# Query-key scores as two weighted fp32r products, their low parts made on VectorE, and four more up tiles ahead of the gates

## The reference, cut to what matters

```python
qry = (xf @ w_q).reshape(t, PEER_HEADS, 2, PEER_HALF)     # 8 heads, two halves of 128
s1 = einsum('thd,hkd->thk', qry[:, :, 0], k1)             # 128 keys each
s2 = einsum('thd,hkd->thk', qry[:, :, 1], k2)
v1, i1 = lax.top_k(s1, 16); v2, i2 = lax.top_k(s2, 16)
cand = v1[..., :, None] + v2[..., None, :]                # 256 per head
top_v, top_c = lax.top_k(cand, 16)
gates = softmax(top_v); idx = e1 * 128 + e2
act = gelu(einsum('phkd,pd->phk', u_tab[idx], xb))
out = einsum('phk,phkd->pd', gates * act, v_tab[idx])
```

## Time and profile before

| what | value |
| --- | --- |
| three runs | 1452.3, 1454.21, 1452.57 us |
| profiled execution, first to last instruction (the page gives no other time of it) | 1451.0 us |
| PE busy | 1443.0 us, 99% |
| DVE, ACT, POOL busy | 77%, 53%, 31% |
| instructions | 22297 |
| HBM traffic | 237 GB/s over the span |

### The profile page before, as it was taken

How to read it: one execution, slowest core, us unless ns; L and a number is a source line. 1 busy time by engine, 2 the same in 40 slices (tenths; PEclk the granted TensorE clock), 3 DMA queues, 4 the chain that set the end, 5 groups by cost and what they waited for, 6 DMA issues and landing times.

```text
span 1451.0 us, 22297 instructions
## 1 busy us (share of the span) xinstructions
PE 1443.0 (99%) x7422; PEld 1202.6 (83%) x7422; DVE 1121.3 (77%) x1929; ACT 767.8 (53%) x1010; POOL 445.1 (31%) x208
## 2 busy tenths in 40 slices
PE   9999999999999999999999999999999999999999
PEld 8888887878788888888888888888888888888887
DVE  5979898876689999996999997355666666666665
ACT  7445787776645455555555555454444444444442
POOL 5867566347457778892000000000000000000000
PEclk9999999999999999999999999999999999999999
DMA  7544534457433666666888888979889888888883
GB/s 241 174 145 145 186 117 155 167 184 265 145 130 121 217 218 214 214 215 215 304 301 306 302 305 298 342 243 323 288 293 288 289 288 291 286 292 284 295 287 140
DMA packets 166708, 345.17 MB, mean 238 GB/s; under 512 B 13421, under 2 KB 78957, under 8 KB 164337
## 3 DMA queue, kind: packets, MB, share of 16 engines
q1 hardware_dynamic: 166640, 344.32, 70.3%
HBM read 268.76 MB, written 75.51 MB: 237 GB/s over the span
## 4 chain that ended last, share of the span: by engine, by line
PE 97%; ACT 1%; DVE 1%; DMA 0%; issue 0%; SPq 0%; ACTq 0%
PE ps L1293 32%; PE ps L1302 32%; PE ps L791 13%; PE ps L814 6%; PE ps L1331 4%; PE ps L1162 3%; PE ps L1001 1%; PE ps L1228 1%; PE ps L779 1%; PE ps L1011 1%; PE ps L1055 1%; PE ps L1235 1%; PE ps L863 1%; PE ps L839 0%; DMA xs<-in_x 0%
## 5 line engine op out<-in xcount | busy, mean ns | idle before, releaser
L1293 PE MATMUL ps<-hT_r,u_r 128*128 128x512 f32 x2048 | 470.3, 390 | 0.0
L1302 PE MATMUL ps<-v_r,w_pairs 128*128 128x512 f32 x2036 | 461.7, 389 | 0.0
L1293 PEld LDWEIGHTS ps<-hT_r,u_r 128*128 128x128 f32 x2048 | 382.8, 188 | 79.1
L1302 PEld LDWEIGHTS ps<-v_r,w_pairs 128*128 128x128 f32 x2036 | 382.1, 188 | 79.4
L2484 DVE TENSOR_TENSOR v_r<-vraw,v_r 128x1024 fp32r<-128x1024 f32 x128 | 156.8, 1225 | 147.3 <-ACT v_r L1804 147.3
L1804 ACT ACTIVATE v_r<-vraw 128x1024 fp32r<-128x1024 f32 x128 | 135.7, 1060 | 253.3 <-PE ps L1302 247.9
L506 POOL TENSOR_TENSOR w_r<-w_raw,w_r 128x1024 fp32r<-128x1024 f32 x85 | 222.6, 2625 | 150.7 <-ACT w_r L1410 104.9
L581 POOL TENSOR_TENSOR u_r<-uraw,u_r 128x1024 fp32r<-128x1024 f32 x60 | 173.3, 2901 | 41.8 <-ACT u_r L1731 41.7
L1750 ACT ACTIVATE act_stage<-ps 128x512 f32<-128x512 f32 x128 | 76.5, 598 | 181.3 <-PE ps L1293 181.2
L1731 ACT ACTIVATE u_r<-uraw 128x1024 fp32r<-128x1024 f32 x128 | 135.3, 1058 | 54.1 <-DMA uraw<-in_u 50.8
L1410 ACT ACTIVATE w_r<-w_raw 128x1024 fp32r<-128x1024 f32 x95 | 100.0, 1059 | 84.5 <-PE ps L814 33.1
(11 more groups left out here) (299 smaller groups left out, 1577.4 us busy)
## 6 DMA issues: line engine op xcount, KB each, us to landing
uraw<-in_u SPq DMA_DIRECT2D x128, 512.0 KB, 4.7
vraw<-in_v SPq DMA_DIRECT2D x128, 512.0 KB, 5.2
w_raw<-in_w SPq DMA_DIRECT2D x100, 512.0 KB, 3.5
acts_out<-act_stage SPq DMA_DIRECT2D x128, 256.0 KB, 2.3
gates<-stage SPq DMA_DIRECT2D x16, 2048.0 KB, 7.4
g_in<-gates SPq DMA_DIRECT2D x64, 512.0 KB, 6.6
act_in<-acts_out SPq DMA_DIRECT2D x128, 256.0 KB, 5.3
gates_pre<-pre_stage SPq DMA_DIRECT2D x24, 256.0 KB, 2.2
```

Of the source, the lines that this page charges most:

```text
L1293: ins = pe.matmul(bank(s % 2), u2[s][:, w, k * P:(k + 1) * P], hr4[:, w, k, :], start=i == 0, stop=i == 15, skip_group_check=True)
L1302: ins = pe.matmul(bank(2 * q + h), w2[:, s, w, q * P:(q + 1) * P], v2[s][:, w, h * BANK:(h + 1) * BANK], start=start and w == 0, stop=stop ...
```

## The change

Six things change.

1. The keys are split once into `keys_hi` (keys / 128, by ACT, two instructions of 1024 columns) and `keys_lo` (keys - 127 x keys_hi, by DVE, in two halves). Each query is split into `q_hi` (127/128 of it, by ACT's old copy with a scale) and `q_lo` (the query minus q_hi, by DVE, read from PSUM: `low_query`).
2. `key_scores` makes for each 128 tokens two fp32r products (q_hi with keys_hi, q_lo with keys_lo) in place of one fp32 product; `score_copy` multiplies by 128. It waits for `qk_lo`, which DVE raises, in place of `pq_out`, which ACT raises.
3. DVE's program has `low_query(2g + 2)` and `low_query(2g + 3)` behind the first list g, for g below 7, and the second half of the keys behind list 2.
4. Scores 14 and 15 stand behind up tiles 0 and 1 in place of before them; the others are spread in pairs over the even items.
5. `N_TOP` goes from 60 to 64, and with it `N_GATE` from 108 to 112: POOL makes the low parts of four more up tiles, and four fewer are left behind the gates. `EXP_AFTER`, `TURN_AFTER` and `EARLY` change, and the second half of the gate table for the second four down tiles is loaded 14 and 15 tiles behind `N_GATE` in place of 15 and 17.
6. POOL writes its index pattern after eight up tiles in place of before the first; three semaphores are shared with others, with the waits raised to match.

```diff
-N_TOP, PER_BLOCK = 60, 12
+N_TOP, PER_BLOCK = 64, 12
-EARLY = (N_GATE + 8, N_GATE + 12, N_GATE + 16)
+EARLY = (N_GATE + 6, N_GATE + 9, N_GATE + 12)
-SCORES_AFTER = {1: (0,), 3: (1, 2), 5: (3, 4), 7: (5, 6), 9: (7, 8), 11: (9, 10), 13: (11, 12), 14: (13,), 15: (14,)}
+SCORES_AFTER = {1: (0,), 2: (1,), 4: (2, 3), 6: (4, 5), 8: (6, 7), 10: (8, 9), 12: (10, 11), 14: (12, 13)}
+LATE_SCORES = (14, 15)
+KEYS_BEHIND = 2
-EXP_AFTER, TURN_AFTER = (12, 24, 36, 49), (23, 36, 48, 56)
+EXP_AFTER, TURN_AFTER = (14, 27, 39, 51), (27, 40, 52, 60)
...
-                elif q in (15, 17):
-                    part_of_g(1, 1, (q - 15) // 2 * NBLK // 2)
+                elif q in (14, 15):
+                    part_of_g(1, 1, (q - 14) * NBLK // 2)
...
-                pe.wait_ge(pq_out, g + 1)
+                pe.wait_ge(qk_lo, g + 2 + (g >= 2 * KEYS_BEHIND + 2))
                 at_least(pe, score_out, g - 1)
                 for t in range(TT):
-                    ins = pe.matmul(bank(4 + s % 2)[:, t * P:(t + 1) * P], qryT3[:, s, t * P:(t + 1) * P],
-                                    keysT3[:, g, :] if isinstance(g, int) else keysT[:, bass.ds(g * NKEYS, NKEYS)],
-                                    start=True, stop=True)
+                    c_ = slice(t * P, (t + 1) * P)
+                    for w, (q_, k_) in enumerate(((q_hi3, keys_hi3), (q_lo3, keys_lo3))):
+                        ins = pe.matmul(bank(4 + s % 2)[:, c_], q_[:, s, c_], k_[:, g, :], start=w == 0, stop=w == 1)
...
             for n in range(N_TOP):
                 up(n, n % 4)
+                if n < len(LATE_SCORES):
+                    key_scores(LATE_SCORES[n], LATE_SCORES[n] % 4)
                 if n in TURN_AFTER:
...
+            def high_keys(h):
+
+                c_ = slice(h * D, (h + 1) * D)
+                act.wait_ge(xa_keys_in, 32)
+                act.activation(keys_hi[:, c_], keysT[:, c_], ACT.Copy, scale=1.0 / SPREAD).then_inc(key_hi, 1)
+
             for n in range(I_PQ + 2, I_PQ + 4):
                 high_w(n, n % 4, back=4)
+            high_keys(0)
...
-                act.activation(qryT3[:, n % 4, :], bank(query_bank(n)), ACT.Copy).then_inc(pq_out, 1)
+                act.activation(q_hi3[:, n % 4, :], bank(query_bank(n)), ACT.Copy, scale=KEEP).then_inc(pq_out, 1)
...
+            def low_query(n):
+
+                dve.wait_ge(pq_out, n + 1)
+                dve.tensor_tensor(q_lo3[:, n % 4, :], bank(query_bank(n)), q_hi3[:, n % 4, :].bitcast(F32),
+                                  ALU.subtract).then_inc(qk_lo, 1)
+
+            low_keys(0)
+            low_query(0)
+            low_query(1)
             for g in range(2 * PH):
                 first_lists(g)
+                if g == KEYS_BEHIND:
+                    low_keys(1)
+                if g < PH - 1:
+                    low_query(2 * g + 2)
+                    low_query(2 * g + 3)
```

More of the change, by code:

```diff
@@ L276, in build @@
         mem_scaled = projT[:, 0:2048].rearrange("p (k t) -> p k t", t=MEM)
-        qryT3 = qryT.rearrange("p (g t) -> p g t", t=T)
         keysT3 = keysT.rearrange("p (g k) -> p g k", k=NKEYS)
+        q_hi3, q_lo3 = (x.rearrange("p (g t) -> p g t", t=T) for x in (q_hi, q_lo))
+        keys_hi3, keys_lo3 = (x.rearrange("p (g k) -> p g k", k=NKEYS) for x in (keys_hi, keys_lo))
         sb_v3 = sb_v.rearrange("p (t c) -> p t c", c=512)
@@ L416, in build @@
         rows_made, if_made, cols_turned, cols_out = sem("rows_made"), sem("if_made"), sem("cols_turned"), sem("cols_out")
-        conv_done, silu_done, x_far = sem("conv_done"), sem("silu_done"), sem("x_far")
+        conv_done, silu_done, far = sem("conv_done"), sem("silu_done"), sem("far")
         normed, qkT_lo, mpT_lo = sem("normed"), sem("qkT_lo"), sem("mpT_lo")
@@ L523, in _ @@
                     pool.tensor_scalar(x_scaled[:, n, :], side_of(xr4[:, 0], k, side).bitcast(F32), SPREAD - 1.0, 1.0,
-                                       ALU.mult, ALU.mult).then_inc(x_far, 1)
+                                       ALU.mult, ALU.mult).then_inc(far, 1)
             for n in range(2, 6):
@@ L574, in _, with low_us @@
             low_ws(I_PQ + 4, ITEMS - I_PQ - 4)
+            def low_us(first, last):
+                for n in range(first, last):
+                    pool.wait_ge(u_hi, n + 1)
+                    pool.tensor_tensor(u2[n % 4][:, 1, :], u_raw[n % 4], u2[n % 4][:, 0, :].bitcast(F32),
+                                       ALU.subtract).then_inc(u_lo, 1)
+            low_us(0, 8)
             pool.wait_ge(w_lo_ready, ITEMS - len(DVE_LOW))
@@ L577, in _ @@
                       allow_small_or_imprecise_dtypes=True).then_inc(const_made, 1)
[L579 to L582, removed]
+            low_us(8, N_TOP)
         @block.sync
@@ L1442, in mem_high @@
                     act.activation(mem_scaled[:, i, :], mr4[:, 0, i, :].bitcast(F32), ACT.Copy,
-                                   scale=SPREAD - 1.0).then_inc(mem_far, 1)
+                                   scale=SPREAD - 1.0).then_inc(far, 1)
             act.wait_ge(xT_out, 2 * KD)
@@ L1724, in score_copy @@
                 at_least(act, score_used, g + 1 - SCORE_SLOTS)
-                act.activation(sc3[:, g % SCORE_SLOTS, :], bank(4 + s % 2), ACT.Copy).then_inc(score_out, 1)
+                act.activation(sc3[:, g % SCORE_SLOTS, :], bank(4 + s % 2), ACT.Copy,
+                               scale=SPREAD).then_inc(score_out, 1)
             def high_u(n, s):
@@ L1740, in query @@
                     high_u(0, 0)
+                    high_u(1, 1)
                 for g in SCORES_AFTER.get(n, ()):
                     score_copy(g, g)
+                if n == 1:
+                    high_keys(1)
             def gelu(n, s):
@@ L1858, in x_low @@
                 n = side * KD + k
-                dve.wait_ge(x_far, n + 1)
+                dve.wait_ge(far, n + 1)
                 dve.wait_ge(xT_hi, n // 2 * 2 + 2)
@@ L1864, in mem_low @@
             def mem_low(k):
-                dve.wait_ge(mem_far, k + 1)
+                dve.wait_ge(far, 2 * KD + k + 1)
                 dve.scalar_tensor_tensor(out=mr4[:, 1, k, :], in0=mem_part(k), scalar=key_cols[:, KD + k:KD + k + 1],
@@ L2410, in take_lists, with low_keys @@
                                   ALU.subtract).then_inc(list_out, 1)
+            def low_keys(h):
+                c_ = slice(h * D, (h + 1) * D)
+                dve.wait_ge(key_hi, h + 1)
+                dve.scalar_tensor_tensor(out=keys_lo[:, c_], in0=keys_hi[:, c_].bitcast(F32), scalar=1.0 - SPREAD,
+                                         in1=keysT[:, c_], op0=ALU.mult, op1=ALU.add).then_inc(qk_lo, 1)
+            def low_query(n):
[5 more added lines that the diff above has]
+            low_query(1)
             for g in range(2 * PH):
                 first_lists(g)
+                if g == KEYS_BEHIND:
[3 more added lines that the diff above has]
+                    low_query(2 * g + 3)
             dve.wait_ge(score_used, 2 * PH)
```

21 lines of the change are left out of this document (10 added, 11 removed).

## The result

The changed kernel takes 1459.2 us (median of 5 runs, 1458.73 to 1462.16), against 1452.3 us (5 runs) for the kernel before on the same chip: ratio 1.0051, 95% interval 1.004 to 1.0062, so slower by 0.4 to 0.6%. The profiled execution took 1458.73 us, its span is 1457.0, 6.0 us more than before. The forecast was 1460.0 us.

The account below looks back on a forecast made before the run. PE was taken to bound the kernel, with 97% of the chain that ended last. Terms 0 + 0.0 + 5.4 + 2.0 = 7.4 us on a span of 1451.0 gave 1458.4; with 1.6 us for the median, 1460.0; range 1452.4 to 1465.0.

Parts of the forecast that it names:

- Scores on PE, nothing: Score products on PE: 128 fp32r products at 0.110 to 0.112 us each, as before; at most 0.3 us gained.
- The first rivals, weights at the bf16 pace: Scores on PE: weight loads at 0.060 us, 6.7 us gained; 1453.3 at 5%, or 1445.9 with no stop at 4%.
- Entry: Before scores 0: splitting the keys and low query 0 delays PE by 0 to 0.3 us.
- Lists 23.9 us later: DVE: list 7 waits for query 15, until 456.7; nine lists follow, conversion at 502.4 against 478.5.
- not the work but the wait: DVE's lists: waiting for queries, not the 13.5 us of added work, costs the whole 23.9 us.
- The second lists: DVE: second lists keep their length, `cand_top` at 522.1; bounds 1.3 us earlier to 4.2 us later.
- The stop, +5.4: Up tile 17: PE waits for gelu 15 behind ACT's late exponent, 518.9 to 524.3, 5.4 us; bounds 4.1 to 9.6.
- Slow restart, +2.0: PE behind the stop: about 4 us of work at half pace lose 2.0 us; bounds 0 and some 3.
- The rival without it: PE behind tile 17: the stop comes without the slow restart, 1458.0 us; chance 24%.
- The later steps are covered: Later turns on PE: list 0 ends at 563.8, its turn comes at 564.3 or later; last turn keeps 8 us.
- Tail nothing: Gates and after: four more tiles in front shift the gates by 14.5 us, without new work for PE.

Follow-up runs that it names:

- e6: Changed kernel with only the first score product of each pair, the product of the low parts left out: 1455.64 us, ratio 1.0019.
- e9: e8 with DVE's second half of the keys behind list 3, not 2, and the low queries reordered to match: 1451.54 us, ratio 0.9988.
- e2: Changed kernel with DVE's low queries spread 1, 2, 1, 2, 1, 1, 2, 1, 1, 2 behind lists 0 to 9: 1453.78 us, ratio 1.0008.
- e3: Changed kernel without the low parts of queries; the second product takes the high query again, scores wait for ACT's copies: 1454.32 us, ratio 1.0009.
- e8: e7 with the low parts of queries and keys stored as bf16: 1453.67 us, ratio 1.0004.
- e1: Changed kernel with the exponents three tiles later, behind gelus 17, 30, 42 and 54, turns unmoved: 1460.64 us, ratio 1.0056.
- e7: Changed kernel with e2's order of low queries, 60 up tiles ahead of the gates, earlier gate loads, exponents and turns moved: 1453.26 us, ratio 1.0006.
- e4: Changed kernel with 60 up tiles ahead of the gates, not 64, and the last turn behind tile 58: 1466.38 us, ratio 1.0095.
- e5: Changed kernel with exponents behind gelus 17, 30, 42, 54 and turns behind tiles 30, 43, 55, 61: 1455.22 us, ratio 1.0019.
- e10: e7 with the second half of the keys one list later and low queries reordered, second product still fp32r: 1454.52 us, ratio 1.001.

## Why the prediction was right

The forecast of 1460.0 stood 0.8 us above the median and its cause was the one that the runs show. That it came so close is in part luck: the span was forecast at 1458.4 and measured 1457.0, and the median lay 2.2 us above it, not 1.6. Step by step:

- **Scores on PE, nothing.** Right. The products start 0.110 us apart, where the earlier trace rows had their like, and the stage took 0.3 us more, not less. e6 puts 0.113 us on each product. That the weight load sets this pace follows from e9 and from the up tiles: there a product of 512 columns starts every 0.227 us, so multiplying 128 columns is worth 0.057 us and cannot be the 0.110. In e9 a bf16 second operand has the shorter load, and the products follow. The groups by form of the changed kernel, weight loads of the scores as long as before:

```profile
L1239 PEld LDWEIGHTS ps<-keys_lo,q_lo 128*128 128x128 f32 x64 | 12.2, 191 | 0.3
L1239 PEld LDWEIGHTS ps<-keys_hi,q_hi 128*128 128x128 f32 x64 | 12.2, 191 | 0.8 <-DVE q_lo L2441 0.4
```

  The first rivals, weights at the bf16 pace, fall with these rows. The Trainium skill (TensorE: Matmul & The Clock Gate, Weight-path perf modes) turns the fast load on for 128 weights of a type other than FP32: the trace agrees for bf16 (0.10 us) and shows that fp32r, at 0.19 us, counts as FP32 there.
- **Entry.** PE waited 0.4 us for q_lo, 0.1 over the bound: the first half of the keys took 1.63 us, not 1.2.
- **Lists 23.9 us later.** 456.5 for list 7 (456.7 predicted) and 502.26 for the conversion (502.4), so 23.8. e2 shows the cause: 14.5 us of it go with the order. The other 9.2 us stay in e2, and 8.1 of them go in e3, which has no low queries. So "not the work but the wait" was too strong: the order made the part of the delay that reached PE, the added work the rest.
- **The second lists.** `cand_top` rose at 520.3, predicted 522.1. The conversion took 0.29 us where I kept 1.78, and the subtraction 0.29, not 0.45. It was the lower bound that held, and a little more: the two gave 1.65 us, the bound was 1.3. I chose the middle value because nothing told which collisions would move.
- **The stop, +5.4.** 4.1 us, at tile 17 as predicted, at the lower bound. It was mis-sized by the second lists' term: that gelu ended at 522.55, not 524.3, while PE came to the wait 0.3 us earlier than forecast and restarted 0.1 us behind the gelu. The rest held: the exponent's start to the gelu's end took 522.55 - 520.33 = 2.2 us, as in the earlier trace rows.
- **Slow restart, +2.0.** 1.5 us: PE ran 3.0 us at the lower clock where I took about 4. In e6 it cost 2.3 us and in e8 1.7. The rival without it falls.
- **The later steps are covered.** Right, but for a further reason: besides the 4.9 us that a stop hands over, ACT's wait kept POOL out of DVE's way, and list 0 ended at 559.4, not 563.8. e1 took the stop away and found 563.5 (in the changed kernel's time) and a wait of 4.9 us.
- **Tail nothing.** 0.5 us, at a load of up weights that I had not looked at. e7, with the tiles and loads of before, does not have it.

The terms were 0 + 0 + 5.4 + 2.0 = 7.4 and measured 0.4 + 4.1 + 1.5 + 0.5 = 6.5 us, of which the profiled execution got 0.6 back before scores 0; the median moved by 6.9.

## What to carry to other kernels

An in-order engine that gets a new small job per item, each with a wait, runs from then on at the pace of the items, even though its busy time hardly grows: count what stands behind the last such wait, not the added work. Follow a delay through every queue to the next table of places, and expect that mending one wait uncovers the next (e1) and that part of the time gained ahead of it is waited away (e6). Before rewriting a product in another type, look at what its weight load costs; with 128 columns in fp32r it was the load that was paid.

## What was not expected of the hardware

- **A wait of ACT speeds DVE up.** It works through POOL: the same candidate sum takes 2.28 or 4.49 us, the low part of 1024 keys 1.21 or 3.06 us. What decides is which of the two starts first. The candidate sum of the changed kernel at 502.47 took its short 2.28 us, and POOL's instruction, begun at 502.68, took 4.33 us where 2.40 is usual; in e8 POOL came first and DVE took the longer time. The low queries, one operand from PSUM, lasted 0.67 to 0.69 us in all 16 instances of the changed kernel. The Trainium skill (SBUF — State Buffer, SBUF: two separate sides) describes this as a lock between a DVE instruction with two SBUF inputs and a GpSimd instruction that reads SBUF, the later one waiting out the whole of the other. The traces agree: each side is held up when it comes second (where the starts lie within 0.1 us the order cannot be read), and the instruction with an operand from PSUM never is.
- **Even short gaps can bring the lower clock, but do not always.** In e8 it fell to the lower level behind a gap of 1.7 us (a wait of 1.47). In e4 and e5, at the one-hots, it stayed full behind waits of 1.44 and 1.22 us, and so it did in every trace behind a wait of 1.6 us in the transposes ahead of the queries; the kernel before, whose clock reads 1.00 from 376 to 386 us:

```profile
381.44 1.71 PE L779 MATMUL ps<-ident,h_scaled 128*128 128x128 f32 x12 [1.60 <-ACT h_scaled L1707]
```

  What makes the difference no run here shows. Near the start of the kernel the lower clock comes in some executions alone; the window from 12 to 16 us shows the full clock in e9 but 0.60 in e10:

```profile
12.00:16.00 4.00, 3.56 (x32) 3.57 (x32) 3.70 (x8) 2.89 (x7) 2.25 (x6) 1.00 1.02 412
```
```profile
12.00:16.00 4.00, 3.96 (x21) 3.96 (x22) 2.92 (x6) 1.46 (x4) 1.11 (x3) 0.60 1.03 410
```

  PE waited 1.9 us for the loads of xs at the start of e9 and 1.3 in e10, so a longer wait there is not what brings it. It costs up to 1.6 us, more than several of the differences argued over here, and it is why e7 and e10, or e2 and e3, are not told apart.
